# mLSTM and S5 hybrid step on Trainium2: rows of u by broadcasting DMA, taps in pairs, y of chunks 4 and 5 as one group, a split slab

## The reference

```python
def trunk(x, mC, mn, mm, sre, sim, p):
    for layer in range(DEPTH):
        h = rms_norm(x, p['norm_mix_g'][layer])
        if layer % N_MIXERS == 0:
            out, C, n, m = mlstm_mixer(h, ...)      # w_in, 8 heads of 64 x 128, w_out
        else:
            out, hr, hi = s5_mixer(h, ...)          # 64 groups of 16, state 64, w_glu
        x = x + out
        x = x + sq_relu_mlp(rms_norm(x, p['norm_ffn_g'][layer]), ffn_w_up, ffn_w_down)
    return rms_norm(x, p['norm_final_g']), new states
# mlstm, a head: weights exp(b_t - b_s + i_s - m_t), causal, on q k^T; then times v; plus decayed state
# s5, a group: y = c h + d u, h_t = a h_(t-1) + b u_t (complex); then gelu, then a * sigmoid(g) of w_glu
```

## Time and profile before

| | |
|---|---|
| median of 3 runs | 1388.52 us (1386.57 to 1388.78) |
| profiled execution, time | 1389.6 us |
| profiled execution, span | 1387.8 us |
| busy PE | 1334.1 us, 96% of the span |
| busy DVE, ACT, POOL | 660.6, 442.6, 367.7 us |
| granted TensorE clock, mean | 0.98 |
| bytes moved by DMA | 119.55 MB, mean 86 GB/s |

### The profile page before, as it was taken

One profiled execution on the slowest core, in us unless ns is written; L12 is line 12 of the kernel. 1 busy time (PEld: TensorE's weight loads), 2 busy tenths in 40 slices (PEclk: granted clock), 3 DMA queues, 4 the chain that ended last, 5 costly groups with the idle time before them and its releaser, 6 DMA issues.

```text
span 1387.8 us, 25466 instructions
## 1 busy us (share of the span) xinstructions
PE 1334.1 (96%) x10119; PEld 1289.9 (93%) x10119; DVE 660.6 (48%) x846; ACT 442.6 (32%) x672; POOL 367.7 (26%) x368
## 2 busy tenths in 40 slices
PE   4999999999999999999999896999999999999998
PEld 3999996779999999999999886999999999999997
DVE  6662333665794573343344693343533433333443
ACT  4311133432342241241341235322521422422423
POOL 3000004433799990000018561122000000000032
PEclk9999998999999999999999997999999999999999
DMA  5233231113332232223224985222222232323231
GB/s 146 62 84 84 76 91 28 53 43 76 92 88 79 78 89 80 87 76 90 76 76 141 155 138 130 85 81 85 77 83 84 76 90 76 91 76 91 76 89 72
DMA packets 239139, 119.55 MB, mean 86 GB/s; under 512 B 35512, under 2 KB 235888, under 8 KB 239088
## 3 DMA queue, kind: packets, MB, share of 16 engines
q1 hardware_dynamic: 238832, 118.78, 32.6%
q10 hardware_dynamic: 256, 0.06, 0.0%
HBM read 108.08 MB, written 10.73 MB: 86 GB/s over the span
## 4 chain that ended last, share of the span: by engine, by line
PE 85%; SPq 5%; DVE 5%; issue 1%; ACT 1%; DMA 1%; POOL 0%; DVEq 0%; ACTq 0%; POOLq 0%
PE ps L310 76%; SPq L521 2%; PE ps L1550 2%; PE ps L1577 2%; SPq L548 1%; DVE wlo L294 1%; DMA d_y<-U 1%; PE ps L1540 1%; PE ps L1586 1%; PE ps L1580 1%; DVE R L331 1%; PE ps L1603 1%; PE ps L1791 1%; SPq L502 0%; DVE xg_lo L360 0%
## 5 line engine op out<-in xcount | busy, mean ns | idle before, releaser
L289 ACT ACTIVATE whi<-raw 128x1024 fp32r<-128x1024 f32 x177 | 187.0, 1057 | 503.3 <-PE ps L310 491.0
L310 PE MATMUL ps<-hid_hi,whi 128*128 128x288 f32 x1408 | 302.9, 296 | 11.5 <-DVE hid_lo L1413 8.9
L310 PE MATMUL ps<-xg_hi,whi 128*128 128x288 f32 x1424 | 306.8, 297 | 3.0 <-DVE wlo L294 1.5
L310 PE MATMUL ps<-xg_lo,whi 128*128 128x288 f32 x1424 | 305.4, 295 | 0.0
L310 PE MATMUL ps<-xg_hi,wlo 128*128 128x288 f32 x1424 | 303.7, 294 | 0.0
L310 PE MATMUL ps<-hid_lo,whi 128*128 128x288 f32 x1408 | 302.0, 295 | 0.0
L310 PE MATMUL ps<-hid_hi,wlo 128*128 128x288 f32 x1408 | 300.7, 295 | 0.0
L294 DVE TENSOR_TENSOR wlo<-raw,whi 128x1024 fp32r<-128x1024 f32 x177 | 251.1, 1418 | 93.1 <-ACT whi L289 92.9
L310 PEld LDWEIGHTS ps<-hid_hi,whi 128*128 128x128 f32 x1408 | 226.0, 189 | 12.9 <-DVE hid_lo L1413 9.4
L310 PEld LDWEIGHTS ps<-xg_hi,whi 128*128 128x128 f32 x1424 | 228.4, 189 | 5.2 <-issue 2.3
L310 PEld LDWEIGHTS ps<-xg_hi,wlo 128*128 128x128 f32 x1424 | 229.0, 189 | 0.0
(11 more groups left out here) (351 smaller groups left out, 1132.1 us busy)
## 6 DMA issues: line engine op xcount, KB each, us to landing
raw<-in_ffn_w_up SPq DMA_DIRECT2D x64, 512.0 KB, 4.0
raw<-in_ffn_w_down SPq DMA_DIRECT2D x64, 512.0 KB, 3.7
raw<-in_mlstm_w_in SPq DMA_DIRECT2D x25, 512.0 KB, 3.8
raw<-in_s_w_glu SPq DMA_DIRECT2D x16, 512.0 KB, 3.9
raw<-in_mlstm_w_out SPq DMA_DIRECT2D x8, 512.0 KB, 3.7
late<-d_taps SPq DMA_DIRECT2D x64, 64.0 KB, 2.8
d_u<-unat SPq DMA_DIRECT2D x8, 288.0 KB, 2.8
U<-d_u SPq DMA_DIRECT2D x16, 144.0 KB, 6.7
```

The lines of the kernel that those rows point to most:

```text
L289: nc.scalar.activation(whi[:, s], raw[:, s], ACT.Copy).then_inc(whi_done, 1)
L310: last = nc.tensor.matmul(ps[:, 2 * s + c, 0:HN], w[:, s, k, :], a[:, k, c * HN:(c + 1) * HN], start=(k == 0 and n == 0), stop=(k == KT - ...
```

## The change

1. **u rows.** `spread` and its PSUM bank are gone. SP stores the 8 x 512 numbers of u to DRAM (`d_ub`), and `load_u_row(h)` reads row h from there onto 128 partitions, into `acc` for even heads and `sqb` for odd ones. Rows 0 and 1 are issued around slab 24, row h+2 in SP's turn h ahead of the wait for that head's new state. `exps` reads the row in SBUF.
2. **States.** `sums` waits for `qblk_ready` and `ncol_ready` only ahead of its last four matmuls. SP loads the state of head h+2 behind the two stores of `Cst` and ahead of the store of `CP`, and doesn't wait for that one.
3. **Output projection.** PE multiplies slab 26 for k = 0 to 3 only, then the two transposes, then slab 25 for k = 7, and then slab 26 for k = 4 to 7.
4. **S5.** A taps load covers two chunks (8 DMAs of 128 KB instead of 16 of 64 KB). The order on SP is taps of pair 0, the second half of u, pairs 1 and 2, stores of the first y group, pair 3. Chunks 4 and 5 of y go as one group. The two GLU slabs are loaded ahead of the stores of chunk 6. Of the eight stores of chunk 7, SP issues four and ACT four, behind its copy of the chunk and ahead of the gelu of chunk 4. `gelu_lo` waits for six answered chunks for k under 4 and for all eight otherwise.

The diff, cut to its core:

```diff
-            def spread(h):
-                if h:
-                    pe.wait_ge(exp_done, h)
-                nc.tensor.matmul(ps[:, 0, :], SEL[:, h, :], qkvo[0:8, 24, TS:N], start=True, stop=True).then_inc(u_done, 1)
...
+            sp.wait_ge(m_ready, 1)
+            sp.dma_start(d_ub, qkvo[0:8, 24, TS:N]).then_inc(ub_out, 16)
+            def load_u_row(h):
+                if h < 2:
+                    sp.wait_ge(ub_out, 16)
+                    sp.wait_ge(acc_done, ACC0[1])
+                else:
+                    sp.wait_ge(exp_done, h - 1)
+                sp.dma_start(Ub[h % 2], d_ub[h:h + 1, :].to_broadcast([P, L])).then_inc(ub_in[h % 2], 16)
             load_slab(sp, 24, 0, slab_in[:, :, 23 * P:24 * P])
+            load_u_row(0)
+            load_u_row(1)
...
-                    sp.wait_ge(c_out[s], 16 * 3 * (h // 2))
+                    sp.wait_ge(c_out[s], 16 * 3 * (h // 2) - 16)
...
             for h in range(H):
                 s = h % 2
+                if h + 2 < H:
+                    load_u_row(h + 2)
                 sp.wait_ge(c_new, h + 1)
...
-                sp.dma_start(p_C[0, 0, h], CP[:, s, :]).then_inc(c_out[s], 16)
                 if h + 2 < H:
                     load_state(h + 2)
+                sp.dma_start(p_C[0, 0, h], CP[:, s, :]).then_inc(c_out[s], 16)
...
+            def load_taps(j):
                 for i in range(T):
+                    sp.dma_start(taps_pair[j][i * GC:(i + 1) * GC],
+                                 d_taps[2 * j * P:(2 * j + 2) * P, i * GC:i * GC + P].rearrange("(g c) m -> c g m", c=GC)).then_inc(mt_in[j], 16)
             load_taps(0)
+            load_u(1)
             load_taps(1)
-            load_u(1)
             load_taps(2)
-            load_taps(3)
-            groups = ((0, 1), (2, 3), (4,), (5,), (6,), (7,))
+        Y_GROUPS = ((0, 1), (2, 3), (4, 5), (6,), (7,))
...
+            for n in range(len(Y_GROUPS)):
+                if n == 3:
                     for i in range(2):
                         load_slab(sp, I_GLU + 2 + i, 0, slab_glu[:, :, P + D * (1 - i):2 * P + D * (1 - i)])
+                store_y(n, range(4) if n == 4 else range(T))
+                if n == 0:
+                    load_taps(3)
                 fetch_y(n)
...
-                act.wait_ge(u_done, h + 1)
+                act.wait_ge(ub_in[h % 2], 16 * (h // 2 + 1))
...
+                    if k == KT - 1:
+                        act.wait_ge(yev_ready, KT)
+                        for n in range(4, T):
+                            act.dma_start(d_y[k * P:(k + 1) * P].rearrange("(g c) t b -> t c g b", c=GC)[n],
+                                          U2[n * GC:(n + 1) * GC, 8 * k:8 * k + 8, :]).then_inc(y7_out, 16)
...
-                dve.wait_ge(sy_done, k - k % 2 + 2)
+                dve.wait_ge(sy_done, 6 if k < 4 else 8)
...
                 pe.wait_ge(p_masked, h + 1)
-                pe.wait_ge(qblk_ready, h + 1)
-                pe.wait_ge(ncol_ready, h + 1)
...
+                pe.wait_ge(qblk_ready, h + 1)
+                pe.wait_ge(ncol_ready, h + 1)
                 for b4 in range(4):
...
-            product(pe, I_OUT + 1, 0, hid, None, range(KT - 1))
+            product(pe, I_OUT + 1, 0, hid, None, range(4))
...
-            for i in range(2):
-                product(pe, I_OUT + i, 0, hid, (hid_ready, 0), (KT - 1,))
+            product(pe, I_OUT, 0, hid, (hid_ready, 0), (KT - 1,))
+            product(pe, I_OUT + 1, 0, hid, None, range(4, KT))
```

More of the change, by code:

```diff
@@ L101, in build @@
         Q4 = xtok[:, 0, 0:N]
+        Ub = (acc[:, 0:L], sqb[:, 0:L])
         LF, LI, AM, BC, MM, GT1, GT2 = range(7)
@@ L538, in _, with store_y @@
-            for n, group in enumerate(groups):
-                for k in group:
-                    if k + 4 < KT:
-                        load_taps(k + 4)
-                if n == 4:
+            def store_y(n, steps):
+                first, last = Y_GROUPS[n][0], Y_GROUPS[n][-1]
+                sp.wait_ge(yev_ready, last + 1)
+                for i in steps:
+                    sp.dma_start(d_y[first * P:(last + 1) * P].rearrange("(g c) t b -> t c g b", c=GC)[i],
+                                 U2[i * GC:(i + 1) * GC, 8 * first:8 * last + 8, :]).then_inc(y2_out[n % 2], 16)
@@ L544, in _ @@
                         load_slab(sp, I_GLU + 2 + i, 0, slab_glu[:, :, P + D * (1 - i):2 * P + D * (1 - i)])
-                first, last = group[0], group[-1]
-                sp.wait_ge(yev_ready, last + 1)
-                for i in range(T):
-                    sp.dma_start(d_y[first * P:(last + 1) * P].rearrange("(g c) t b -> t c g b", c=GC)[i],
-                                 U2[i * GC:(i + 1) * GC, 8 * first:8 * last + 8, :]).then_inc(y2_out[n % 2], 16)
+                store_y(n, range(4) if n == 4 else range(T))
@@ L1610, in _ @@
             last.then_inc(us_done, 1)
-            spread(0)
             scores(0)
-            spread(1)
             pe.wait_ge(us_arg, 1)
```

38 lines of the change are left out of this document (20 added, 18 removed).

## The result

| | kernel before | changed kernel |
|---|---|---|
| time, median of 12 runs each | 1388.28 us | 1379.61 us |
| range of the runs | 1385.95 to 1390.31 | 1376.84 to 1384.40 |
| ratio, 95% interval | | 0.9943, 0.9930 to 0.9957 |
| profiled execution, its span | 1389.6, 1387.8 | 1380.89, 1378.6 |

What follows compares the result with a forecast made beforehand. Slab matmuls on PE take three quarters of the span, so gains come only from PE's other work and idle time: 0.8 + 4.3 + 4.0 + 2.4 + 9.2 = 20.7 us off 1388.5 gives 1367.8; range 1362 to 1377.

Steps and rivals of the forecast that it cites:

- Part 1, u rows: Attention loop: u rows by DMA replace the spread matmul on PE; 4.3 us from five heads, 0.8 at the start.
- the slower rival: Attention heads: broadcast row lands late, each microsecond beyond 4.6 adding to every head; 1394 us at 9 us landing, chance 0.05.
- Part 2, head 7: Head 7's sums: PE starts 2.3 us earlier and full clock gives 1.7 more; 4.0 us in all.
- Part 3, out-projection: Ahead of slab 27: half of the second slab follows the first slab's end and covers PE's wait; gain 2.4 us.
- Part 4, the end of the stage: S5 stage, chunk 7's copy at 846.5 to second GLU slab at 857.5: fewer SP issues, y of chunk 7 barely in time.
- Part 4, the front: S5 stage up to chunk 7's copy: PE's 1.1 us wait for taps goes; copy at 846.5 instead of 847.63.
- taps bound by data: S5 stage: fewer, larger issues only fill the queue, chunk 2's taps come later, 3 of 9.2 us stay; 1374 us, chance 0.15.
- the forecast of 0: From the second GLU slab to the kernel's end: no change in time, 0 us.
- the slow start of the second slab: Behind 866.71, at the second GLU slab: 1.2 us more gain if all ran at full clock, only in the upper end.

Runs made afterwards that it cites:

- sums_waits_back: `taps64` with the waits for `qblk_ready` and `ncol_ready` again ahead of all of a head's sums; 1372.34 us, ratio 0.9882.
- filler64: `taps64` with identity transposes that nobody reads in four short waits of PE; 1374.53 us, ratio 0.9894.
- order64_filler: `filler64` with chunk 2's taps, but not chunk 3's, issued ahead of U's second half; 1371.48 us, ratio 0.9889.
- split_back: `taps64` with the second out-projection slab as before the change; 1374.62 us, ratio 0.9911.
- bygroup: `taps64` with each 64 KB taps DMA writing one group of channels into all 128 partitions; 1377.68 us, ratio 0.9920.
- taps64_pairwait: `taps64` with PE waiting for both chunks of a pair before the first of them; 1379.14 us, ratio 0.9929.
- filler_wait: Changed kernel with 28 transposes that nobody reads in PE's wait at chunk 2; 1374.96 us, ratio 0.9899.
- att_only: Kernel before with only the attention and out-projection changes, S5 stage as before; 1378.03 us, ratio 0.9924.
- iorder64: `taps64` with the eight DMAs of taps and U issued in step order 0, 1, 4, 5, 2, 3, 6, 7; 1375.15 us, ratio 0.9901.
- taps64: Changed kernel with taps loaded and waited for one chunk at a time again, in 64 KB DMAs; 1371.79 us, ratio 0.9886.

## Why the prediction was wrong, point by point

- **Part 1, u rows.** Right. Five head periods gave 3.90 (sums of head 1 to head 6: 52.84 before, 48.94 after), forecast 4.3; the start gave 1.02, forecast 0.8. The six rows took 3.2 to 4.2 us to land, median 3.6, between the bounds of 2.9 and 6.7 and under the 4.6 that PE would have noticed, so the slower rival did not come.
- **Part 2, head 7.** Right in size: 3.78, of which 2.14 less waiting and 1.64 in the twenty sums at full clock; forecast 4.0. The forecast rested on the later waits (2.3 us earlier "even if the load comes no earlier"); by `sums_waits_back` the earlier load does nearly all of it here.
- **Part 3, out-projection.** Right: 2.37, forecast 2.4.
- **Part 4, the end of the stage.** Right: the forecast put 11.0 us between chunk 7's copy (846.5) and the second GLU slab (857.5), and it is 10.99 after 19.08. The margin is thin, as the prediction said ("barely"): in `filler64`, `order64_filler`, `split_back` and `bygroup` PE waits up to 2.3, 2.2, 2.2 and 5.0 us for `hid_lo`, and the end takes 13.1 to 16.4.
- **Part 4, the front: the step that failed.** It reads "Chunks: taps cost PE one wait of 1.1 us; it goes", and put chunk 7's copy 1.1 us earlier. It came 14.4 later. Three errors are in that one line. First, the pace: the sum took 0.47 us per issue as the queue's limit, from 16 issues, and dismissed the data rate though the row of 32 has 0.59 each; that was the queue waiting for its transfers. Second, the wait for a pair: PE waited for one chunk before and two after, which the part never put against the bytes ahead, 2.75 MB and 3.28 MB; `taps64_pairwait` shows the landing 4 us later by this alone and a cost of 4 to 7 us, and the larger form adds 2.5 to the landing. Third, the clock: a wait of 4.4 us was followed by 12 us at half clock, and filling it gave back 6.8 us of the stage (`filler_wait`). Part 2 had counted this very effect at head 7, and part 4 did not count it. Together they account for the 8.6 us around chunk 2. The other 5.8 us, 3.5 in chunks 0 and 1 and 2.3 in chunks 6 and 7, are for the most part half clock too, and their cause stays open.
- **The rival "taps bound by data"** had the mechanism and the place (chunk 2), at 1374 and a chance of 0.15. It took 6 of the 9.2 us away; the miss was 15.5, since the rival took the delay of the bytes and left out the pair and the clock.
- **The order on SP.** In the text on the change, U's second half is said to have moved ahead of the second pair. Counted in chunks nothing moved there: before, chunks 0 and 1, U, chunks 2 to 5; after, pair 0, U, pairs 1 and 2. The last pair's loads stood behind the first stores before too; they moved ahead of the first fetch of y.
- **Outside the change.** The 1.7 us ahead of the attention are no effect: over the sixteen profiled executions that stretch takes 200.4 to 203.0 us, whatever the edits. Behind the stage it is otherwise, and here the forecast of 0 was wrong. From the second GLU slab to the end of the span it is 521.1 us before and 518.3 after, and the other runs fall into the same two sets: 518.2 to 518.5 in the eight others whose end took at most 11.2 us, 521.1 to 521.2 in `bygroup`, `filler64` and `order64_filler` (520.5 in `att_only`; `iorder64` with 518.9 and an end of 12.2 lies near the first set, and `split_back` with 518.2 and an end of 15.4 falls out of the pattern). So the early end brings up to 2.8 us more. Of these 1.2 are the slow start of the second slab, which the prediction had only at its upper end; why the rest comes at the kernel's very end is open. In this profile the change's own gain is then 11.1 - 6.3 + 2.8 = 7.6.

What stays open is what sets the clock in the stage's first chunks. `att_only` has the stage of the kernel before and no wait for taps, and its front is 72.6 us against 69.1, all of it clock: PE idles less (5.5 us against 7.35) and is busy longer (67.1 against 61.8) at 0.82 against 0.91. Open is also what of the 7.8 us between `taps64` and the changed kernel the profile owes to its own run, since the same stage took 81.5 us in `taps64`, 87.9 in `sums_waits_back` (a wait of 1.7 for taps at chunk 2) and 84.1 in `split_back`. There is little slack at chunk 2 with single chunks either: in `taps64` PE comes to it late enough because chunks 0 and 1 ran partly at half clock.

## What to carry to other kernels

When transfers are merged, ask what the waiting engine waits for: a semaphore for two pieces is late by the second piece's bytes, and a count of the bytes ahead of each wait, at the us per MB that one measured wait gives, shows that before the kernel is built. Take a queue's pace from its longest run of issues, not the shortest; more per issue than the short run shows means that the data set it. Price the half clock behind a new wait of TensorE, and not only the wait: the one of 4.4 us here cost about 11, an estimate from its length and the 6.8 us that filling it gave back, while the one of 1.07 us in the kernel before was followed by full clock. And don't expect filler work to pay unless the data behind it is early.

## What the runs showed of the hardware

- Merging 64 KB transfers into 128 KB ones made the bytes no faster: 3.28 MB were there after 30.2 us in the small form and after 32.3 to 33.2 in the large, and issues on the full queue went from 0.59 to 1.06 us. The Trainium skill, DMA: Bandwidth & Descriptors, section "Rules for kernel authors", advises to merge many small transfers into a large one; here that saved issues on a queue that was not short of them.
- The same 64 KB written as 128 rows of 512 B took 0.62 us per issue, as 16 partitions of eight such pieces 0.47.
- 28 matmuls without a reader, 3.22 us of them, in a wait made the changed kernel 4.7 us faster.
- Behind two waits of 1.94 and 1.67 us, close together, 32 matmul records of `block_sums` took 2.21 us, at half clock; with fillers in these waits (`filler64`) the same took 1.27.
